# Projecting a memory's keys and values in halves of 128 columns, the values with the weights as the moving operand

## The reference

```python
mem_kv = _rms_norm(mem, g_mem) @ w_mem_kv          # (256 x 1024) @ (1024 x 1024)
mk, mv = jnp.split(mem_kv, 2, axis=-1)             # keys, values: 4 heads of 128
es = jnp.einsum('bshd,bmhd->bhsm', eq, mk) * (XATTN_HEAD_DIM ** -0.5)
ep = jax.nn.softmax(es, axis=-1)
eo = jnp.einsum('bhsm,bmhd->bshd', ep, mv)
```

## Time and profile before

| what | value |
|---|---|
| median of 3 runs | 3904.89 us (3898.66 to 3904.95) |
| the profiled execution's own time | 3904.89 us |
| its span in the profile | 3903.0 us |
| PE busy | 3478.7 us, 89% |
| POOL busy | 1576.6 us, 40% |
| DVE busy | 1806.0 us, 46% |
| ACT busy | 907.2 us, 23% |

### The profile page before, as it was taken

The page is one execution under the profiler, slowest core; times in us unless marked ns, Lnnn a source line. Parts: engine busy times, 40 slices in busy tenths (PEclk is TensorE's granted clock), DMA queues, the critical chain, the costliest instruction groups (busy, mean ns, idle before and its releaser), DMA issues.

```text
span 3903.0 us, 43114 instructions
## 1 busy us (share of the span) xinstructions
PE 3478.7 (89%) x16180; PEld 2777.8 (71%) x16180; DVE 1806.0 (46%) x2344; ACT 907.2 (23%) x1689; POOL 1576.6 (40%) x2013
## 2 busy tenths in 40 slices
PE   7997999978988999979899698889859988989988
PEld 6777888867766667767677477777747766678867
DVE  5763323246794554643521646574543433222343
ACT  3232112121112442323112222222211112110021
POOL 3544832204683225534453254243314433334523
PEclk9999999979999999989899899899979999999999
DMA  3122321102122012121121110000102101111211
GB/s 111 52 70 63 108 65 55 54 6 79 54 79 73 25 28 68 38 92 41 45 87 49 57 44 28 22 28 28 29 12 81 49 27 38 46 57 36 79 38 65
DMA packets 300658, 205.30 MB, mean 53 GB/s; under 512 B 25749, under 2 KB 277657, under 8 KB 300473
## 3 DMA queue, kind: packets, MB, share of 16 engines
q1 hardware_dynamic: 271241, 132.77, 12.3%
q10 hardware_dynamic: 29232, 69.95, 4.9%
HBM read 173.06 MB, written 29.63 MB: 52 GB/s over the span
## 4 chain that ended last, share of the span: by engine, by line
PE 61%; DVE 15%; ACT 4%; POOL 3%; issue 2%; PEld 1%; ACTq 1%; DMA 1%; PEldq 0%; DVEq 0%; POOLq 0%
PE ps L343 45%; PE ps L1321 4%; PE ps L793 3%; DVE wrk L659 3%; POOL w_lo L2512 2%; ACT wrk L821 2%; PE ps L806 1%; POOL w_hi L2507 1%; PE ps L1692 1%; PE ps L532 1%; PE ps L2024 1%; DVE wrk L846 1%; DVE small L849 1%; PE ps L356 1%; PE ps L685 1%
## 5 line engine op out<-in xcount | busy, mean ns | idle before, releaser
L2507 POOL TENSOR_TENSOR w_hi<-w_raw,pool_one 128x256 fp32r<-128x256 f32 x1004 | 685.9, 712 | 2274.0 <-PE ps L343 2241.5
L343 PE MATMUL ps<-h_hi,w_hi 128*128 128x512 f32 x2928 | 1208.4, 413 | 92.0 <-POOL w_lo L2512 23.9
L343 PE MATMUL ps<-h_lo,w_hi 128*128 128x512 f32 x2928 | 1156.9, 395 | 0.0
L343 PE MATMUL ps<-h_hi,w_lo 128*128 128x512 f32 x2928 | 1156.2, 395 | 0.0
L2512 POOL TENSOR_TENSOR w_lo<-w_raw,w_hi 128x256 fp32r<-128x256 f32 x1004 | 891.7, 917 | 23.2
L343 PEld LDWEIGHTS ps<-h_hi,w_hi 128*128 128x128 f32 x2928 | 559.7, 191 | 270.1 <-issue 103.2
L343 PEld LDWEIGHTS ps<-h_hi,w_lo 128*128 128x128 f32 x2928 | 559.0, 191 | 121.6
L343 PEld LDWEIGHTS ps<-h_lo,w_hi 128*128 128x128 f32 x2928 | 560.8, 192 | 113.3 <-issue 9.1
L343 PE MATMUL ps<-y_hi,w_hi 128*128 128x512 f32 x704 | 290.4, 413 | 30.7 <-issue 29.9
L343 PE MATMUL ps<-y_hi,w_lo 128*128 128x512 f32 x704 | 277.7, 395 | 0.0
L343 PE MATMUL ps<-y_lo,w_hi 128*128 128x512 f32 x704 | 277.5, 394 | 0.0
(11 more groups left out here) (343 smaller groups left out, 3815.6 us busy)
## 6 DMA issues: line engine op xcount, KB each, us to landing
w_raw<-in_w_in SPq DMA_DIRECT2D x87, 512.0 KB
w_raw<-in_even_w_in SPq DMA_DIRECT2D x48, 512.0 KB
away<-wrk ACTq DMA_DIRECT2D x80, 256.0 KB, 2.0
wrk<-away ACTq DMA_DIRECT2D x32, 512.0 KB
w_raw<-in_odd_w_in SPq DMA_DIRECT2D x32, 512.0 KB
wrk<-in_x ACTq DMA_DIRECT2D x16, 512.0 KB, 8.2
w_raw<-in_w_br SPq DMA_DIRECT2D x32, 256.0 KB
w_raw<-in_even_w_out SPq DMA_DIRECT2D x24, 256.0 KB
```

The source lines that it names most:

```text
L343: mm = nc.tensor.matmul(ps[:, b, 0:n], w[:, slot, k, :], rhs(part, k, b), start=(k == 0 and q == 0), stop=(k == nk - 1 and q == 2))
L2507: ins = nc.gpsimd.tensor_tensor(hi, raw, one[:, 0:2], ALU.mult)
```

## The change

The function `memory_tile` goes; memory tiles use the ordinary `dense_run`, with n = 128. A tile is now made of two halves of 128 memory rows, half b in bank b, each of 24 matmuls with 128 moving columns. For the keys the weights stay stationary. For the values the operands are swapped: the memory is stationary and the weights move, so that the result has the memory rows on the partitions. ACT copies half b as soon as it is there, the values to another place of the same buffer, and the stages "values turned" are gone. The planned duration of a memory stage becomes `AHEAD_PACE * dense_us(r, P)` = 41.6 instead of 26.4.

```diff
-MEMORY_TILE = 3.3
...
     def rhs_of_memory(which):
-        return lambda part, k: mem_view((y_hi, y_lo)[part], which)[:, k, :]
+        return lambda part, k, b: mem_view((y_hi, y_lo)[part], which)[:, k, b * P:(b + 1) * P]
+    keys_of = [rhs_of_memory(0), rhs_of_memory(1)]
+    values_of = [rhs_of_memory(0), rhs_of_memory(1)]
+    weights_moving = values_of
...
             for q, (w, part) in enumerate(((w_hi, 0), (w_hi, 1), (w_lo, 0))):
-                mm = nc.tensor.matmul(ps[:, b, 0:n], w[:, slot, k, :], rhs(part, k, b), start=(k == 0 and q == 0),
+                l, r = w[:, slot, k, :], rhs(part, k, b)
+                if rhs in weights_moving:
+                    l, r = r, l
+                mm = nc.tensor.matmul(ps[:, b, 0:n], l, r, start=(k == 0 and q == 0),
                                       stop=(k == nk - 1 and q == 2))
...
-    def memory_tile(pe, t, bank, rhs, first):
...
-    def memory_kv(name, w_kv, which, first):
+    def memory_kv(name, w_kv, which):
...
+            rhs = (keys_of, values_of)[kind][which]
+
+            def f_pe(pe, r=r, rhs=rhs):
                 pe.wait_ge(mem_normed.sem, mem_normed.nth(0))
-                for j in range(r.n):
-                    pe.wait_ge(tiles_split, r.t0 + j + 1)
-                    yield j / r.n
-                    for part in memory_tile(pe, r.t0 + j, j % 2, rhs, first and (kind, j) in ((0, 0), (0, 1))):
-                        yield (j + part) / r.n
+                yield from dense_run(pe, r, rhs, rhs, P)
...
                 for j in range(r.n):
-                    yield (j + 1) / r.n
-                    out_ready(act, r.t0 + j, 1)
                     for b in range(2):
-                        nc.scalar.activation(wt(10)[:, j * MEM + b * P:j * MEM + (b + 1) * P],
-                                             ps[:, j % 2, b * P:(b + 1) * P], ACT.Copy).then_inc(dense_free[b], 1)
-                    act.wait_ge(dense_free[0], r.t0 + j + 2)
-                    act.wait_ge(dense_free[1], r.t0 + j + 2)
+                        yield when(r, j, b)
+                        out_ready(act, r.t0 + j, b)
+                        dst = wt(10)[:, j * MEM + b * P:j * MEM + (b + 1) * P] if kind == 0 else \
+                            wt(10)[:, b * HALF + j * P:b * HALF + (j + 1) * P]
+                        nc.scalar.activation(dst, ps[:, b, 0:P], ACT.Copy).then_inc(dense_free[b], 1)
+                        act.wait_ge(dense_free[b], r.t0 + j + 2)
...
-            stage(name, AHEAD_PACE * MEMORY_TILE * r.n, ("pe",), pe=f_pe, act=f_act)
+            stage(name, AHEAD_PACE * dense_us(r, P), ("pe",), pe=f_pe, act=f_act)
...
-        def v_turn(pe):
-            for m in range(2):
-                for h in range(4):
-                    nc.tensor.transpose(ps[:, 6 + m, h * P:(h + 1) * P],
-                                        wt(vt)[:, h * MEM + m * P:h * MEM + (m + 1) * P], ident)
-
-        def v_copy(act):
-            for m in range(2):
-                nc.scalar.activation(wt(vt, m), ps[:, 6 + m, :], ACT.Copy)
-        stage(tag + " values turned", 1.0, pe=v_turn)
-        stage(tag + " values turned", 1.5, act=v_copy)
```

More of the change, by code:

```diff
@@ L1130, in _hybrid @@
                           lambda j: ACT.Identity if j < 4 else ACT.Sigmoid)
-    def memory_kv(name, w_kv, which, first):
+    def memory_kv(name, w_kv, which):
         at = next_away[0]
         next_away[0] += 2
-        rhs = rhs_of_memory(which)
         for kind in range(2):
             r = run(2, *both(w_kv, kind * W))
-            def f_pe(pe, r=r, kind=kind):
+            rhs = (keys_of, values_of)[kind][which]
+            def f_pe(pe, r=r, rhs=rhs):
                 pe.wait_ge(mem_normed.sem, mem_normed.nth(0))
-                for j in range(r.n):
-                    pe.wait_ge(tiles_split, r.t0 + j + 1)
-                    yield j / r.n
-                    for part in memory_tile(pe, r.t0 + j, j % 2, rhs, first and (kind, j) in ((0, 0), (0, 1))):
-                        yield (j + part) / r.n
+                yield from dense_run(pe, r, rhs, rhs, P)
             def f_act(act, r=r, kind=kind):
+                ch = chains["act"]
                 for b in range(2):
@@ L1151, in f_act @@
                 for j in range(r.n):
-                    yield (j + 1) / r.n
-                    out_ready(act, r.t0 + j, 1)
                     for b in range(2):
-                        nc.scalar.activation(wt(10)[:, j * MEM + b * P:j * MEM + (b + 1) * P],
-                                             ps[:, j % 2, b * P:(b + 1) * P], ACT.Copy).then_inc(dense_free[b], 1)
-                    act.wait_ge(dense_free[0], r.t0 + j + 2)
-                    act.wait_ge(dense_free[1], r.t0 + j + 2)
+                        yield when(r, j, b)
[4 more added lines that the diff above has]
+                        act.wait_ge(dense_free[b], r.t0 + j + 2)
                 for b in range(2):
                     send(act, away[at + kind, :, b * HALF:(b + 1) * HALF], wt(10, b), b)
-            stage(name, AHEAD_PACE * MEMORY_TILE * r.n, ("pe",), pe=f_pe, act=f_act)
+            stage(name, AHEAD_PACE * dense_us(r, P), ("pe",), pe=f_pe, act=f_act)
         return at
-    at_kv = [memory_kv("E k v", weights("w_mem_kv"), 0, True),
-             memory_kv("even k v", weights("even_w_mem_kv_2"), 1, False),
-             memory_kv("odd k v", weights("odd_w_mem_kv_2"), 1, False)]
+    at_kv = [memory_kv("E k v", weights("w_mem_kv"), 0), memory_kv("even k v", weights("even_w_mem_kv_2"), 1),
+             memory_kv("odd k v", weights("odd_w_mem_kv_2"), 1)]
     def swapped(w, first):
```

## The result

The change makes the kernel slower by 0.57%: 3927.24 us (median of 5 runs, 3917.27 to 3930.4) against 3903.03 (5 runs), ratio 1.0057 with a 95% interval of 1.0046 to 1.0068, that is 18 to 27 us. Forecast were 3909 us and a range to 3923, with "no change" (0.50) likelier than "slower" (0.42). The profiled execution of the changed kernel took 3922.88 us (its span 3921.1), that of before 3904.89: +18.0.

What follows compares the result with a forecast made beforehand. PE was taken to bound the kernel beside dense work, with chunk 7 able to swallow more. First section -0.3, tail +7.9 and values turned -3.5 gave +4.1 on 3904.9, so 3909 us, range 3896 to 3923.

Steps and rivals of the forecast that it cites:

- the price of a matmul: Memory tiles: a 128-column float32r matmul costs 0.115 us, bounds 0.102 and 0.120, against 0.120 for 256 columns.
- the double price: Rival, memory matmuls: 128 columns run as plain float32 in two records, 0.225 us each; +127 us, 4036 us; chance 10%.
- POOL falls out of the bound: Memory chunks: POOL's split needs 6.1 us a tile where a tile lasts 9.6, so POOL no longer holds the pace.
- chunk 7 takes work in: End of first section: dense work now reaches over chunk 7, filling PE's idle time at clock near 1.00, still 66 us.
- the tail: Behind chunk 7: four last pieces of E q, 5.5 us, and ACT's write wait, 3.7, delay the next section: +7.9 us.
- so the memory chunks become like chunks 4 and 5: Chunks 1 to 3: 332 matmuls x 0.115 plus 28.3 us for the chunk itself, 66.5 us a chunk, bound by PE.
- The rest of the section: From the end of the memory to the chunks' end: 3.98 chunks x 66.3 = 263.9 us, plus chunk 3's surplus of 4.5.
- the turning of the values: Three attentions: dropping three times 8 transposes, scores slightly earlier; -3.5 us, bounds -2.8 and -13.6.
- The sum: Whole kernel: -0.3 + 7.9 - 3.5 = +4.1 us against the profiled 3904.9, so 3909 us.
- 63 us of new work and the idle chunk 7: First section: 63 us more PE work and chunk 7's idle, low-clock time cancel, 499.0 us against 499.3: -0.3 us.

Runs made afterwards that it cites:

- plan-tail kernel: The kernel before with only the planned duration of a memory stage at 40.0 instead of 26.4: 3886.32 us, ratio 0.995.
- plan-only kernel: The kernel before with only the planned duration of a memory stage raised from 26.4 to 41.6: 3872.77 us, ratio 0.9921.
- Streamed twice: The changed kernel with each of the 1152 memory matmuls moving its operand twice, 256 columns instead of 128: 3911.05 us, ratio 1.0016.
- late-wait kernel: The changed kernel with ACT's wait for the previous stage's write moved to just ahead of the first copy into that buffer half: 3919.47 us, ratio 1.0036.

## Why the prediction was wrong

**Right: the price of a matmul, and the double price excluded.** 0.113 us at the full clock, forecast 0.115. The count of records shows one per matmul.

**Right: POOL falls out of the bound, chunk 7 takes work in, the tail.** The tail from the chunk's last product (864.44 us, just ahead of ACT's 864.50) to L606 at 873.33 is 8.9 us, forecast 9.2. What the forecast of the tail left out is the clock behind it: after PE's wait of 3.85 us it is low from 874.5 to 877.9, which adds some 1.7 us. Chunk 7 with its dense work ended 62.1 us after its start (864.4 - 802.3), even below the 66.3. ACT's wait is paid where it was placed, and the plan-tail kernel, without it, is 7 us shorter in that stretch than the plan-only kernel.

**Wrong: "so the memory chunks become like chunks 4 and 5", 66.5 us each.** This step took a price measured at the full clock and a clock of 1.00. Measured are 81.3, 69.8 and 69.8: 220.9 us for the three instead of 199.5, +21.4. The mean clocks give the time at 1.2 GHz: 2 x (0.17 x 81.3 + 0.07 x 69.8 + 0.07 x 69.8) = 47 us, and at half the clock half of it is lost, 24 us. The forecast's own terms then close: 3 x (28.3 + 332 x 0.113) + 24 = 221 us. Streamed twice, the same matmuls in the same order had some 3 us at the low clock and took 207.1, though each costs 7 ns more: 3 x (28.3 + 332 x 0.120) and 1.7 for the clock make 206. So the sum of a chunk was right, and the full clock that it took for granted was not.

That narrow matmuls keep the clock down is shown by two kernels that differ in the columns only, and by the stretches behind equal waits. The two banks and the swapped operands are the same in both kernels, so they are not the cause. That a wait of PE starts the fall is shown by the late-wait kernel for one dip; the dips at the chunks' starts always have such a wait close ahead, but taking it away was not tried. In the kernel before the waits at the starts of chunks 1 to 3 were no shorter (3.78, 1.70 and 3.29 us instead of 1.87, 1.11 and 1.78), with 256 columns, or 512 in chunk 3, and these chunks had 0.95, 1.00 and 0.98. Why narrow matmuls keep the clock low is open.

The Trainium skill (TensorE: Matmul & The Clock Gate, HAM oscillation) puts a falling clock down to gaps in PE's work. The trace agrees on what starts it: the four falls of the changed kernel in chunks 1 to 3 begin within a wait of PE (at 437.6 us within the one of 2.85) or 1.5 us behind it. It shows besides that PE's work after the wait counts: with records that fill every microsecond the clock was back after 3.4 us at 256 columns and after 13.7 at 128.

**The rest of the section** came out 6.4 us better: chunks 4 to 7 took 265.6 us to the last product instead of 269.7 (263.9 + 4.5, and 1.3 for the end of the memory), and chunk 0 72.5, where its part was 74.8. It began 0.5 us later. Together 21.4 - 6.4 + 0.5 = 15.5 us above the forecast, and the chunks' end moved by 15.1 (864.4 against 849.3), where -0.3 was forecast. With the tail L606 begins 22.8 us late, forecast 7.6.

**Mis-sized: the turning of the values.** The term was -3.5; taking the turning away from the kernel before gave 0.9975, -5 to -15 us. In the changed kernel the lateness fell from 22.8 at L606 to 18.1 at the end, only 4.7 us. But that is a net figure. The same instructions can be compared in the two traces across each attention; here POOL's split of a weight tile, ahead of the even attention and behind it, first in the kernel before, then in the changed one:

```profile
3053.24 0.80 POOL L2512 TENSOR_TENSOR w_lo<-w_raw,w_hi 128x256 fp32r<-128x256 f32 x1
3174.42 2.12 POOL L2512 TENSOR_TENSOR w_lo<-w_raw,w_hi 128x256 fp32r<-128x256 f32 x3
...
3076.34 1.95 POOL L2488 TENSOR_TENSOR w_lo<-w_raw,w_hi 128x256 fp32r<-128x256 f32 x2
3194.97 1.43 POOL L2488 TENSOR_TENSOR w_lo<-w_raw,w_hi 128x256 fp32r<-128x256 f32 x2
```

The lateness falls from 23.1 to 20.55 us there. Across E's attention it falls from 25.4 (at 1691 us) to 21.8 (at 1887), and across the odd one from 21.0 (3668) to 18.0 (3820): 9.1 us in all. The kernel without turning gains 8.9 us over the same three stretches, the late-wait kernel 9.1, the one that streams twice only 5.3. The plan-only and the plan-tail kernel, which still turn the values, gain 0.9 and lose 1.8, which shows the uncertainty of such a sum. So the term should have been about -9. The difference to 4.7 is lateness that came in elsewhere: 1.7 us from L606 to 895 us (the clock behind the tail) and 2.7 in the rest.

**The sum.** L606 is 15.2 us later than forecast, and the end, 18.0 instead of 4.1, is 13.9 later: the 1.3 between them is the turning's larger gain less those losses. The median of the changed kernel lies another 4.4 us above its profiled execution.

**A sum that hid two large terms.** I let 63 us of new work and the idle chunk 7 cancel, as one step. They came with two edits. The plan alone is worth -31 us (0.9921), and the form of the matmuls costs the stretched kernel 1.0057 - 0.9921 = 1.36%, 53 us: of this -10 are the turning, so about +63 for the matmuls and their clock. That this equals the 63 us of added PE work is chance: the clock is in it too, and a part of the work fills time in which PE stood idle in the plan-only kernel (21.0 us in its chunks 1 to 3, 9.0 in the changed one). Each could have been forecast apart, and the rival with a chance of its own should have been the clock.

**A version that beats both**: the kernel before, with 256 columns and one bank a tile, and only the planned duration at 41.6: 3872.77 us, 0.9921 (0.9905 to 0.9937). At 40.0 with the late wait it is 3873.25, 0.9917.

## What to carry to other kernels

Before splitting a matmul into two of half the columns, look at what PE's weight loads and its clock make of it: here a 128-column float32r matmul cost 0.113 us where one of 256 cost 0.120, and after waits of 1.1 to 2.9 us PE stayed at half its clock for 10 to 17 us. When an edit changes both the work and the planned time, run each alone: the plan was the gain here (-31 us) and hid most of the loss. A merged order has to be read again after any shift of the plan: 9.6 us in the plan made chunks 2 and 3 together 15 us longer. And a term is measured between the same instructions of two traces, not from the difference of the ends.

## What the runs showed of the hardware that was not expected

The granted clock depends on more than PE's busy time. With PE busy for 10.00 of 10.00 us, 49 records of narrow matmuls, it stood at 0.50; the kernel with twice the columns in each had 88 records in the same 10 us at 1.00. And more work was faster: 8 us of added columns (1152 x 7 ns) took 16 us off.
